# Sixteen experts with two request groups: gate and up turned round, the short group in column tiles, the last norm inside the last expert

## What is computed

```python
N_EXPERTS, D_MODEL, D_FF = 16, 1024, 2816
cap = 2 * n // N_EXPERTS                      # 32 rows of the short request, 128 of the long one
aff = softmax(x @ w_router);  gates, idx = top_k(aff.T, cap)
for e in range(N_EXPERTS):
    xe = x[idx[e]]
    ye = (silu(xe @ w_gate[e]) * (xe @ w_up[e])) @ w_down[e]
    out[idx[e]] += gates[e][:, None] * ye
y = layer_norm(ALPHA * x + out, ln2_g, ln2_b)
```

## Time and profile before

| | us |
|---|---|
| median of 3 runs | 3234.73 (3226.6 to 3236.34) |
| the profiled execution, its own time | 3216.33 |
| its span in the profile | 3214.5 |
| experts: first product to last | 911 to 3146 |
| after the last product of the experts | 68.5 |

### The profile page before, as it was taken

How to read it: one execution, slowest core, us unless ns; L and a number is a source line. 1 busy time by engine, 2 the same in 40 slices (tenths; PEclk the granted TensorE clock), 3 DMA queues, 4 the chain that set the end, 5 groups by cost and what they waited for, 6 DMA issues and landing times.

```text
span 3214.5 us, 49626 instructions
## 1 busy us (share of the span) xinstructions
PE 3054.3 (95%) x20206; PEld 2589.6 (81%) x20206; DVE 2126.3 (66%) x2666; ACT 1635.3 (51%) x2020; POOL 172.2 (5%) x183
## 2 busy tenths in 40 slices
PE   7999999999269999999999999999999999999995
PEld 6998777777268979798797978879797887979882
DVE  2430255444777778787777877778787777878774
ACT  2202466532046556555565656556565565656552
POOL 0100000000000000000000000000000000000005
PEclk8999899999679999999999999999999999999997
DMA  4100100112356969779797887969788796977972
GB/s 145 40 27 14 51 26 25 65 73 99 119 180 216 300 227 280 258 230 290 230 299 231 257 277 231 292 221 303 237 246 279 230 300 219 301 244 235 282 235 110
DMA packets 500623, 636.87 MB, mean 198 GB/s; under 512 B 22532, under 2 KB 394244, under 8 KB 500356
## 3 DMA queue, kind: packets, MB, share of 16 engines
q1 hardware_dynamic: 490464, 610.61, 58.6%
q0 software_dynamic: 6144, 20.98, 2.9%
q10 hardware_dynamic: 3788, 2.12, 0.3%
HBM read 607.99 MB, written 25.62 MB: 197 GB/s over the span
## 4 chain that ended last, share of the span: by engine, by line
PE 92%; DVE 4%; POOL 1%; issue 1%; DMA 1%; ACT 1%; ACTq 0%; POOLq 0%; DVEq 0%
PE banks L586 33%; PE banks L588 13%; PE banks L426 11%; PE banks L623 6%; PE banks L631 6%; PE banks L624 5%; PE banks L625 5%; PE banks L493 4%; PE banks L482 2%; PE banks L474 2%; PE banks L473 2%; PE banks L578 1%; DMA b_s<-in_gmlp_b_s 1%; DVE top L1080 1%; DVE top L1079 1%
## 5 line engine op out<-in xcount | busy, mean ns | idle before, releaser
L903 DVE TENSOR_TENSOR w_parts<-raw_units,w_parts 128x1024 fp32r<-128x1024 f32 x1056 | 1292.0, 1224 | 525.4 <-ACT w_parts L833 512.2
L833 ACT CAST w_parts<-raw_units 128x1024 fp32r<-128x1024 f32 x1056 | 1108.8, 1052 | 766.0 <-PE banks L588 466.8
L586 PE MATMUL banks<-xs_parts,w_parts 128*128 128x320 f32 x5632 | 1462.4, 349 | 4.9 <-ACT ys_prompt L822 4.9
L588 PE MATMUL banks<-xs_parts,w_parts 128*128 128x160 f32 x5632 | 1333.0, 237 | 0.0
L586 PEld LDWEIGHTS banks<-xs_parts,w_parts 128*128 128x128 f32 x5632 | 1060.6, 188 | 31.3 <-issue 17.9
L588 PEld LDWEIGHTS banks<-xs_parts,w_parts 128*128 128x128 f32 x5632 | 1078.6, 192 | 0.0
L623 PE MATMUL banks<-w_parts,h_parts 128*128 128x512 f32 x704 | 295.9, 420 | 0.0
L624 PE MATMUL banks<-w_parts,h_parts 128*128 128x512 f32 x704 | 275.8, 392 | 0.0
L625 PE MATMUL banks<-w_parts,h_parts 128*128 128x512 f32 x704 | 275.4, 391 | 0.0
L623 PEld LDWEIGHTS banks<-w_parts,h_parts 128*128 128x128 f32 x704 | 131.9, 187 | 156.1 <-issue 119.9
L631 PE MATMUL banks<-raw_units,hidden 128*32 128x512 f32 x1408 | 204.1, 605 | 0.0
(11 more groups left out here) (157 smaller groups left out, 2348.0 us busy)
## 6 DMA issues: line engine op xcount, KB each, us to landing
raw_units<-in_w_gate SPq DMA_DIRECT2D x352, 512.0 KB, 7.1
raw_units<-in_w_up SPq DMA_DIRECT2D x352, 512.0 KB, 6.9
raw_units<-in_w_down SPq DMA_DIRECT2D x352, 512.0 KB, 4.4
win_raw<-in_w_in SPq DMA_DIRECT2D x10, 1024.0 KB, 5.1
relT<-rel_bias SPq DMA_DIRECT2D x8, 960.0 KB, 4.5
x_rows<-x SPq DMA_DIRECT2D x10, 512.0 KB, 2.6
acc_rows<-ax SPq DMA_DIRECT2D x10, 512.0 KB, 2.6
acc_tiles<-acc_rows SPq DMA_DIRECT2D x10, 512.0 KB, 4.0
```

What stands on the lines that cost most here:

```text
L586: nc.tensor.matmul(bank[:, 0:2 * SLOTS], w_parts[:, HI, u % SPLIT, cols], moving(slice(HI, LO + 1)), start=first, stop=False)
L588: return nc.tensor.matmul(bank[:, 0:SLOTS], w_parts[:, LO, u % SPLIT, cols], moving(HI), start=False, stop=last_one)
L833: nc.scalar.copy(w_parts[:, HI, u % SPLIT, :], raw[:, u % RING, :]).then_inc(s_hi, 1)
L903: return nc.vector.tensor_tensor(out, whole, high.bitcast(F32), ALU.subtract)
```

## The change

**Gate and up.** The roles are exchanged for the long request: its 128 rows (high or low) are stationary, and the weights move, 512 wide (five chunks of 512 and one of 256 make the 2816). Each block of 128 rows of a weight's chunk takes three matmuls (L594 to L596 of the changed file) into one bank. The sum of the parts is then complete in PSUM, and `both` with its `reduce_sum` is gone. The order of the units is now gate, up, gate, up with eight units to a chunk.

**Short request.** Its 32 rows (`xs_short`) are stationary too, in unsplit float32, and meet the raw weights. The four column groups take four quarters of a chunk, with gate and up side by side in one bank: 256 moving columns for each group. This runs for four units at a time (`BATCH_ENDS`), in a row of 16 matmuls (32 instructions on the array). In down each group now takes a quarter of the output columns (256 wide), so that no partial sums are left, and `sum_groups` is gone.

**Turning the product.** The hidden values of a chunk come out with rows on partitions. PE turns them eight units later (`hidden_transposes`, five transposes for a chunk of 512), and ACT and DVE split them.

**The ring.** `raw` has 14 slots instead of 11. A unit is free only after the short request's batch that uses it, also in gate and up, so that the slots are freed four at a time.

**Experts' rows.** The indices are used where they lie (no copies on POOL). Before the first gather DVE makes the row numbers of the quarters for the short request's scatter.

**The end.** In the last expert POOL fetches the ten tiles of `acc_rows` (5 slots), and their norm runs beside it: statistics and bias on DVE, 1/sigma and gain on POOL, normalising and stores on ACT, one tile every four units from unit 20 on. After the last product only the 128 + 32 rows of the last expert are added, normalised and written over the stored rows by two indirect transfers.

The diff, cut to its core:

```diff
-RING = 11
+RING = 14
+CHUNKS = [(c, min(CHUNK, FF - c)) for c in range(0, FF, CHUNK)]
+BATCH_ENDS = [*range(3, 40, 4), 41, 43, *range(47, UNITS, 4), UNITS - 1]
+TURN_AT = [8 * c + 15 for c in range(NC - 2)] + [47, 51]
+FIN_AT = range(20, 60, 4)
...
-            def raw_free(e, u):
-                if u < GU_UNITS:
-                    sp.wait_ge(s_lo, e * UNITS + (u + 1))
+                if u in FIRST_OF_BATCH:
+                    sp.wait_ge(s_raw, e * NB + FIRST_OF_BATCH[u] + 1)
...
-                nc.tensor.matmul(bank[:, 0:2 * SLOTS], w_parts[:, HI, u % SPLIT, cols], moving(slice(HI, LO + 1)),
-                                 start=first, stop=False)
-                return nc.tensor.matmul(bank[:, 0:SLOTS], w_parts[:, LO, u % SPLIT, cols], moving(HI), start=False, stop=last_one)
+                for i, k in enumerate(ks):
+                    w_hi, w_lo = (w_parts[:, part, slot, i * n:(i + 1) * n] for part in (HI, LO))
+                    nc.tensor.matmul(out, xs_parts[:, HI, k, :], w_hi, start=k == 0, stop=False)
+                    nc.tensor.matmul(out, xs_parts[:, LO, k, :], w_hi, start=False, stop=False)
+                    last = nc.tensor.matmul(out, xs_parts[:, HI, k, :], w_lo, start=False, stop=k == KT - 1)
...
+            def short_gate_up(e, end):
...
+                    for i, k in enumerate(ks):
+                        for g in range(4):
+                            last = nc.tensor.matmul(psum[32 * g:32 * g + 32, short_bank(e, c), 0:n // 2].rearrange("p (j f) -> p j f", j=2),
+                                                    xs_short[:, k, :],
+                                                    raw[:, slot:slot + 2, i * n + g * (n // 4):i * n + (g + 1) * (n // 4)],
+                                                    start=k == 0, stop=k == KT - 1)
+                last.then_inc(s_raw, 1)
...
+                for i in range(n // P):
+                    nc.tensor.transpose(psum[:, gate_bank, i * P:(i + 1) * P], hid[:, c % 2, i * P:(i + 1) * P], ident)
+                nc.tensor.transpose(psum[0:n // 4, up_bank, 0:P], hid_p[:, c % 2, 0:n // 4], ident).then_inc(s_hT, 1)
...
+                for f in range(first, end - GU_UNITS + 1):
+                    for g in range(4):
+                        last = nc.tensor.matmul(psum[32 * g:32 * g + 32, short_bank(e, NC), 0:QUARTER], h_short[:, f, :],
+                                                raw[:, (e * UNITS + GU_UNITS + f) % RING, g * QUARTER:(g + 1) * QUARTER],
+                                                start=f == 0, stop=f == FT - 1)
...
+            for i in range(TILES):
+                t = fin[:, i % FIN_RING]
+                link(final_rstd(i, i, P))
+                nc.gpsimd.tensor_scalar(nmr[:, i:i + 1], mv[:, i, 0:1], rstd[:, i:i + 1], -1.0, ALU.mult, ALU.mult).then_inc(s_frs, 1)
+                pool.wait_ge(s_norm, i + 1)
+                nc.gpsimd.tensor_tensor(t, t, ln2_g, ALU.mult).then_inc(s_gain, 1)
+                if 2 <= i < TILES - FIN_RING + 2:
+                    pool.wait_ge(s_out[i - 2], 16)
+                    fetch(i - 2 + FIN_RING)
```

More of the change, by code:

```diff
@@ new lines, in down @@
+            def down(e, f):
+                slot = (e * UNITS + GU_UNITS + f) % SPLIT
+                if f % 4 == 0:
+                    pe.wait_ge(s_hid, e * NC + f // 4 + 1)
+                if f == 0:
+                    pe.wait_ge(s_hid, e * NC + NC - 2)
+                    pe.wait_ge(s_hp, e * NC + NC - 2)
+                for h_part, w_part in ((HI, HI), (HI, LO), (LO, HI)):
+                    for half in range(2):
+                        last = nc.tensor.matmul(psum[:, pair(e, NC)[half], :], h_parts[:, h_part, f, :],
+                                                w_parts[:, w_part, slot, half * 512:half * 512 + 512],
+                                                start=f == 0 and (h_part, w_part) == (HI, HI), stop=f == FT - 1 and h_part == LO)
+                last.then_inc(s_unit, 1)
@@ L1098, in _ @@
[L1098 to L1104 removed]
+                nc.vector.tensor_copy(gates[:, g, :], psum[:, 0, c])
+                nc.vector.tensor_copy(idx[:, g, :], psum[:, 1, c])
@@ new lines, in _ @@
+            for i in range(FIN_RING):
+                fetch(i)
+            pool.wait_ge(s_ln2, 32)
+            for i in range(TILES):
+                t = fin[:, i % FIN_RING]
+                link(final_rstd(i, i, P))
[5 more added lines that the diff above has]
+                    fetch(i - 2 + FIN_RING)
```

619 lines of the change are left out of this document (308 added, 311 removed).

## The result

The changed kernel takes 3057.93 us (median of 4 runs, 3038.36 to 3115.18) against 3235.53 us of the kernel before (4 runs, 3226.6 to 3245.08): a ratio of 0.9416, with a 95% interval of 0.9373 to 0.9459. The forecast was 3110 us with a range of 3075 to 3190. Ratios are taken without the executions in which the granted clock was lower for longer, as in the one of 3115 us. The profiled execution of the changed kernel took 3055.43 us, with a span of 3053.6.

A forecast was written before the change was run, and what follows sets the result against it. PE was taken to bound the experts, with PE half idle in the end after them. Terms -91 (experts) - 2 (no turning in the last) - 1.4 (front) + 22 (last expert) - 53 (end) = -125, from 3234.7 to 3110 us; range 3075 to 3190.

The forecast's parts named there:

- What bounds the kernel: Experts: PE busy in every microsecond at full clock, so time is the sum of distances between PE starts, plus the end.
- The price of a block of the short request: Gate and up: 0.48 us a block, 0.44 streaming plus 0.02 stagger between passes; a batch of m blocks 0.28 + 0.48 m.
- An expert: Sum of PE's work in one expert: 134.0 us, 5.7 less than 139.7, 91 us over sixteen.
- The last expert: Norm beside it: POOL's gain multiply and small operations exclude DVE's two-input operations, 27 us; net +22 us.
- Both signs: Forecast wrong if PE shows gaps at chunk starts (`s_hid`, `s_mul_p`) or the clock falls below 1.00 in the experts.
- The end: After the last product: 15.5 us in place of 68.5, so -53 us, between -46 and -57.
- The front: Before the first gather: copy and its semaphore wait go, DVE gets small operations; net -1.4 us, between -2 and +1.
- The first: Rival, last expert: no exclusion on DVE, 3088 us; chance 14%.
- The second: Rival, last tiles: POOL's fetch waits for a store, a tile takes 15 us instead of 11; +40, 3150 us; 5%.
- The third: Rival: ring runs dry once an expert when scatter and gather queue with four loads; +80, 3190 us; 7%.
- The fourth: Rival: weight loads of each next block uncovered, 5.6 us an expert; +90, 3200 us; 8%.
- the fifth: Rival: both passes' weight loads uncovered in the long batches, 13.2 us an expert; +211, 3321 us, slower; 6%.

The follow-up runs named there:

- narrow: Changed kernel with each short-request matmul in gate and up cut into four of a quarter of the columns; 3147.57 us (one run).
- after_again: The changed kernel itself, unedited, run again for comparison on one chip; 3070.35 us (6 runs), ratio 0.9355.

## Why the prediction was right and wrong

**What bounds the kernel**: right up to the last expert. PE is full, the casts wait for it and not for weights, and the sum of PE's distances is the time of an expert.

**The price of a block of the short request**: the step that failed. The prediction added 0.02 us a pass for the groups' stagger, taken from the 0.05 by which a quad is longer than one group. But 0.05 is paid once, when the groups start after each other, and not again at each pass. The measured batches make a straight line: 1.00 us for two blocks, 1.87 for four, 3.59 for eight (1514.23 to 1517.82), 0.56 for one. That is 0.14 + 0.431 m, and 0.431 is what the columns' streaming takes: 1024 column times of (0.2275 - 0.12)/256 = 0.42 ns. The lower bound that I had (0.44) was the value, and the choice was made for the row next to it. Ten batches come to 10 x (0.32 - 0.2275 + 1.864 + 0.11) = 20.7 us instead of 22.0, the narrow ones to 2.4 instead of 2.7, down's to 11.5 instead of 12.2: 2.3 us an expert, 37 in all, the largest part of the miss.

**Durations read with two decimals**: a 512-wide matmul takes 0.2275 us, as twelve of them show (1499.78 to 1502.51 in the timeline of `narrow`), not 0.230. In the sum for before that stood 132 times, in the one for now 372 times, so it doesn't cancel: 0.6 us an expert. Turning and the rows' transposes were 0.35 too dear each: their entries were counted and cost nothing apart.

**An expert**: 54.6 + 5.8 + 20.7 + 2.4 + 30.0 + 11.5 + 3.05 + 1.75 = 129.8 by measured prices, and 130.1 measured. Forecast 134.0, and 139.7 for before, where it is 139.3 (the 139.7 also held the four microseconds before the first product). The error of 3.5 us in the difference, 9.2 instead of 5.7, is 56 us in sixteen experts. With 13 us less in the last expert than forecast and 5 more at the end the stretches come to 64 us; the medians show 53 of them. The range gave an expert "1 us shorter or 2 longer", narrower than its own bounds: the lower bound of a block alone takes 40 x 0.04 and 22 x 0.04 off, 2.5 us an expert or 40 in all, which would have reached 3070.

**The last expert**: +22 forecast, +9 measured (some 11 in the second execution). The exclusion was right, shown by leaving POOL's gain out and by moving it to DVE. Its size was off: 16 us of delay on DVE, not 27, since a meeting costs what is left of POOL's operation and not all of it. How the delay reaches PE was not in the sum. That set DVE's total against PE's; what counted was DVE's lead at one place, the start of down, and 2 us of the loss are the clock after that wait. Both signs that the prediction named for being wrong, a gap at `s_hid` and a clock below 1.00 in the experts, came there, in this one expert.

**The end**: 20.5 us where 15.5 was forecast. DVE's chain was right (3032.21 to 3044.07 is 11.9 us; the sum says 11.6, though its terms add up to 11.4, and with the rest to 14.9 instead of 15.5). The last lines of the timeline:

```profile
3032.04 1.07 PE L648 MATMUL banks<-raw_units,h_short 128*32 128x256 f32 x16
3032.21 1.41 DVE L1203 SCALAR_TENSOR_TENSOR xs<-banks,gates,xs 128x512 f32<-128x512 f32 x2 [3.86 <-issue]
...
3042.79 1.27 DVE L1195 SCALAR_TENSOR_TENSOR xs_prompt<-xs_prompt,rstd,ln 32x1024 f32<-32x1024 f32 x1
3044.35 0.88 POOL L1304 DMA_INDIRECT y_prompt<-xs_prompt,idx  x1 [0.60 <-DVE xs_prompt L1195]
```

The last issue ends at 3045.2, and the span 8.4 us later. From 3048 on no engine works and nothing is transferred. The forecast had 3.9 for the landing and nothing for this rest; in the kernel before 5.2 us lie between the end of the last issue (3209.3) and the end of the span, and the 68.5 holds them.

**The front**: the -1.4 can't be seen in the whole, since the clock ahead of the experts moves the first product by tens of microseconds from one execution to the next. The stretch it speaks of shows it: from the start of the last `MATCH_REPLACE8` of the choice to the first product it is 19.9 us before (895.16 to 915.03) and 18.7 now (923.56 to 942.30), 1.1 less.

**The rivals.** The first (no exclusion) fell: the exclusion is there, and its time, 3088, was nearer to the result by chance. The second: the ten tiles' statistics start every 9.5 us in the mean (2925.52 to 3010.71) and never more than 12.7 apart, not 15. The third, a ring that runs dry, fell for the middle experts: PE stayed full even with ten slots. The fourth and the fifth, uncovered loads, fell most clearly: with four times the loads a batch grew by 0.05 us. The Trainium skill (page TensorE: Matmul & The Clock Gate, section The mechanism) has the rule that a load overlaps only with matmuls of other row groups. The trace disagrees: here all share the rows, a pass starts every 0.056 us and loads are listed with 0.110.

## What to carry to other kernels

A cost read from a short row (a first, a last, an entry) is paid once for a sequence until a longer one shows it again: before multiplying it by a count, ask whether it recurs, and if no row can say, keep the value without it in the range with its whole multiple. What a batch costs to enter and leave (0.34 to 0.42 us here) is worth collecting: batches twice as long took another 3.3 us off each expert, until the ring was too short for them where transfers were dense. And work that is put beside a full stretch has to fit in each interval in which it recurs, not only in the sum. Look for the place where the full engine needs something that stands late in the loaded engine's program: here the start of down, where PE waited 3.3 to 5.0 us in every kernel that kept the ten tiles' whole norm beside the last expert, but for the three in which the short request's batches take PE longer (1.9 us in one, none in two). A kernel in which that split stands earlier wasn't run.

## What was new about the hardware

- Weight loads of column groups didn't show at all: four groups with 64 moving columns each make a pass every 0.056 us, though each load is listed with 0.110. One group alone, with a load for each pass of 256 columns, took 0.216 us a pass as well.
- Matmuls of another column group started while, by the counts, four passes of the group before, which stand ahead of them in the program, hadn't started; programmed strictly one after the other, four groups still took 4.5 us a batch and not 6.9.
- With 24576 small matmuls and their loads in place of 6144, PE stopped for up to 4.6 us at a time with nothing awaited; instruction traffic had gone from 2.77 to 5.13 MB.
- With PE equally full, the granted clock between 350 and 450 us was 0.88 in one execution and 0.57 in another, and the first product came at 915 and at 942 us. In `after_again` PE was busy in every microsecond from 450 to 550 us at 0.50; in the first execution of the same kernel it was so at 1.00.
- A wait of 4 us on PE was followed by products at half the clock: the 24 products behind it took 2.1 us more.
